# Weight differences of the seven-pass down product made in other passes, with stores and closing loads moved between queues

## The reference, cut to what matters

```python
def conv_ffn(h, w_up, conv_w, conv_b, w_down):
    u = h @ w_up
    val, gate = u[..., :FFN_HIDDEN], u[..., FFN_HIDDEN:]      # FFN_HIDDEN = 2816
    gate = depthwise_conv(gate, conv_w, conv_b)
    return (jax.nn.silu(gate) * val) @ w_down                 # [tokens, 2816] @ [2816, 1024]
```

## Time and profile before

| | |
|---|---|
| median of 3 runs | 3294.82 us (3293.86 to 3299.07) |
| the profiled execution | 3293.83 us, its span 3291.7 us |
| PE busy | 3143.3 us (95%) |
| VectorE, ScalarE, GpSimd busy | 2085.7 us (63%), 1451.2 us (44%), 666.6 us (20%) |
| mean granted clock of TensorE | 0.983 of full speed |
| DMA | 421.59 MB, mean 128 GB/s |

### The profile page before, as it was taken

The page is one execution under the profiler, slowest core; times in us unless marked ns, Lnnn a source line. Parts: engine busy times, 40 slices in busy tenths (PEclk is TensorE's granted clock), DMA queues, the critical chain, the costliest instruction groups (busy, mean ns, idle before and its releaser), DMA issues. The chain is left out here.

```text
span 3291.7 us, 48901 instructions
## 1 busy us (share of the span) xinstructions
PE 3143.3 (95%) x19182; PEld 2707.4 (82%) x19182; DVE 2085.7 (63%) x2504; ACT 1451.2 (44%) x2491; POOL 666.6 (20%) x770
## 2 busy tenths in 40 slices
PE   7999898899999999999898999999999999999897
PEld 5888777788999999777787778888887788888786
DVE  4999767556755655588544335555554676776687
ACT  5121456465332333344565325555554433333444
POOL 0001000121222222133222101111111222332233
PEclk8999999899999999999999999999999999999999
DMA  6224686533122122666633743422212232222765
GB/s 216 71 88 151 198 267 224 175 102 86 55 77 78 57 76 74 205 212 198 215 131 131 257 161 65 110 51 56 55 45 71 88 80 84 78 82 85 270 198 202
DMA packets 284052, 421.59 MB, mean 128 GB/s; under 512 B 90217, under 2 KB 188457, under 8 KB 282801
## 3 DMA queue, kind: packets, MB, share of 16 engines
q1 hardware_dynamic: 272272, 375.47, 36.8%
q0 software_dynamic: 11552, 43.01, 3.5%
HBM read 324.26 MB, written 94.13 MB: 127 GB/s over the span
## 5 line engine op out<-in xcount | busy, mean ns | idle before, releaser
L2137 DVE TENSOR_TENSOR ring_lo<-raw_rows,ring_hi 128x512 fp32r<-128x512 f32 x200 | 182.7, 914 | 203.4 <-ACT ring_hi L1995 203.1
L1281 PE MATMUL banks<-y_hi,ring_hi 128*128 128x384 f32 (+2 forms) x688 | 221.9, 323 | 4.8 <-DVEq L2125 4.0
L1283 PE MATMUL banks<-y_hi,ring_lo 128*128 128x384 f32 (+2 forms) x688 | 221.8, 322 | 0.0
L1282 PE MATMUL banks<-y_lo,ring_hi 128*128 128x384 f32 (+2 forms) x688 | 221.6, 322 | 0.0
L4584 DVE TENSOR_REDUCE mla_neg_max<-mla_scores 128x1 f32<-128x1280 f32 x128 | 190.1, 1485 | 45.6 <-PE mla_scores L90 45.6
L4554 ACT ACTIVATE mla_e<-mla_scores,mla_neg_max 128x1280 f32<-128x1280 f32 x128 | 169.9, 1327 | 110.4 <-DVE mla_neg_max L4584 110.4
L4496 PE MATMUL mla_turned<-ident,mla_e 128*128 128x128 f32 x1280 | 206.2, 275 | 1.9 <-ACT mla_pt L4562 1.3
L4496 PEld LDWEIGHTS mla_turned<-ident,mla_e 128*128 128x128 f32 x1280 | 156.1, 140 | 48.1 <-issue 11.8
L1281 PE MATMUL banks<-differences,ring_hi 128*128 128x512 f32 (+2 forms) x560 | 192.0, 343 | 3.4 <-ACT sums L2005 2.6
L1283 PE MATMUL banks<-differences,ring_lo 128*128 128x512 f32 (+2 forms) x560 | 191.8, 342 | 0.0
L1282 PE MATMUL banks<-differences,ring_hi 128*128 128x512 f32 (+2 forms) x560 | 191.8, 342 | 0.0
(11 more groups left out here) (537 smaller groups left out, 9093.1 us busy)
## 6 DMA issues: line engine op xcount, KB each, us to landing
raw_rows<-in_ffn_w_up SPq DMA_DIRECT2D x88, 512.0 KB, 3.6
da_ada_w<-in_ada_w SPq DMA_DIRECT2D x10, 4096.0 KB, 14.4
raw_rows<-in_ffn_w_down SPq DMA_DIRECT2D x66, 512.0 KB, 3.7
raw_rows<-in_ffn_w_down SPq DMA_DIRECT2D x88, 256.0 KB, 3.2
out_raw<-scratch_act SPq DMA_DIRECT2D x66, 256.0 KB, 3.7
home_hi<-scratch_act SPq DMA_DIRECT2D x55, 256.0 KB, 3.5
scratch_act<-conv_lines SPq DMA_DIRECT2D x22, 512.0 KB, 4.1
scratch_act<-out_raw SPq DMA_DIRECT2D x22, 512.0 KB, 4.5
```

What stands on the lines that cost most here:

```text
L1281: pe.matmul(out, w_hi[:, w], b_hi[:, a:a + n], start=start and k == 0, stop=False, skip_group_check=True)
L1282: pe.matmul(out, w_hi[:, w], b_lo[:, a:a + n], start=False, stop=False, skip_group_check=True)
L1283: mm = pe.matmul(out, w_lo[:, w], b_hi[:, a:a + n], start=False, stop=k == KD // 2 - 1, skip_group_check=True)
L2137: dve.tensor_tensor(blocks(begun.lo(r)), source(r), blocks(begun.hi(r)).bitcast(F32), ALU.subtract)\
```

## The change

- The difference W12 - W11 is made in P1 and not in P5: P1 loads whole rows (512 KB), P5 loads no weights. W21 minus P6's difference is made in P4 itself, in place in the loaded buffer: P3 loads 256 KB of W22, P4 loads 256 KB of W21. Weight loads of a layer's passes go from eight to seven blocks a pair. A buffer loaded in P1 is free again when GpSimd has made its difference.
- The two last activation stores are issued by GpSimd, before its differences of steps 2 and 3, with a signal of their own (`last_stored`).
- First layer: gain, gate and x loads at j = 40 and 42, one column load in each of steps 44 to 48, the column and gate products on GpSimd at j = 54 and not 33. The next weights are loaded by GpSimd: two blocks when it comes to j = 60, then one behind each of its splits, which come every fourth step from j = 72 on and not every second from 80 on.
- Second layer: the row loads at j = 45, their product at 50, one x load in each of steps 56 to 58; the first two statistics on GpSimd at j = 71 and 72.
- ScalarE's waits in the rest count half steps (`rest_done`); the copies of the c21 block to SBUF come every fourth step of the rest; homes and activation buffers lie elsewhere.

```diff
-    def load(self, sp, s, raw, first, last):
+    def load(self, eng, s, raw, first, last):
         for k in range(first, last):
             if k >= self.RING:
-                sp.wait_ge(s.next_ready, k - self.RING + 1)
-            sp.dma_start(self.place(raw, k), self.w[k * P:(k + 1) * P, :])\
+                eng.wait_ge(s.next_ready, k - self.RING + 1)
+            eng.dma_start(self.place(raw, k), self.w[k * P:(k + 1) * P, :])\
               .then_inc((s.next0_in, s.next1_in)[k % self.RING], 16)
...
+    def load_gain(self, sp):
+        sp.dma_start(self.gates[:, :], row(self.post_gain)).then_inc(self.signals.gain_in.sem, 16)
+
+    def load_column(self, sp, n):
+
+        if n < 4:
+            to, of = self.cols[:, n // 2, n % 2, :], (self.scale_rows, self.shift_rows)[n % 2][n // 2]
+        else:
+            to, of = self.gain_col[:, :], self.pre_gain
+        sp.dma_start(to, column(of), allow_slow_non_contiguous=True).then_inc(self.signals.cols_in.sem, 16)
...
-    SUMS = (P5, P6, P7, P3)
+    ACT_SUMS = (P5, P6, P7, P3)
+    WEIGHT_SUMS = (P1, P6, P7, P4)
...
+    def act_sums_upto(self, j):
+
+        return sum(self.part(i) in self.ACT_SUMS for i in range(j + 1))
+
+    def weight_sums_upto(self, j):
+
+        return sum(self.part(i) in self.WEIGHT_SUMS for i in range(j + 1))
...
-        if self.part(j) == self.P4:
+        part = self.part(j)
+        if part == self.P5:
             return None
-        return j if j < self.steps else j - self.pairs
+        return j if part == self.P1 else j - self.pairs
 
     def step_of_load(self, n):
-        return n if n < self.P4 * self.pairs else n + self.pairs
+        return n if n < self.pairs else n + self.pairs
...
-        row = 2 * q + (part in (self.P6, self.P2, self.P3))
-        if part in (self.P5, self.P3):
-            return row, 0, 2 * BANK
-        return row, BANK if part == self.P6 else 0, BANK
+        if part == self.P1:
+            return 2 * q, 0, 2 * BANK
+        return 2 * q + (part != self.P7), BANK if part in (self.P6, self.P3) else 0, BANK
...
-        if j == 14:
+        if j == 45:
             tail.load_rows(sp)
-        if j == 24:
+        if j == 55:
             tail.rows_used(sp)
-            for t in range(3):
-                tail.load_x(sp, t, self.x_old(t))
+        if 56 <= j < 59:
+            tail.load_x(sp, j - 56, self.x_old(j - 56))
...
-        if j == 18:
+        if j == 50:
             self.tail.prepare_rows(dve)
...
     def gpsimd(self, pool, s, j):
-        pass
+        for t in range(2):
+            if j == self.begins + 5 + t:
+                self.tail.post_gpsimd(pool, t)
 
     def gpsimd_end(self, pool, s):
-        for t in range(self.tiles):
+        for t in range(2, self.tiles):
...
-    EVERY = 2
-
...
-        self.first = down.steps
-        self.tile0 = 6 * down.pairs + 5
+        self.homes_free, self.stores = homes_free, stores
+        self.begins = 6 * down.pairs
+        self.splits = self.begins + 3
+        self.tile0 = self.begins + 4
...
-        if j == 3:
-            latents.load_columns(sp)
-        if j == 14:
+        if j == 40:
+            latents.load_gain(sp)
             latents.load_gate(sp, self.lines[0][:, 0:D])
+        if j == 42:
             latents.load_x(sp, self.lines[1][:, 0:D])
-        k, left = divmod(j - self.first, self.EVERY)
-        if left == 0 and 0 <= k < KD:
-            self.following.load(sp, s, self.raw, k, k + 1)
+        if 44 <= j < 49:
+            latents.load_column(sp, j - 44)
...
-        k, left = divmod(j - self.first - 2, self.EVERY)
+        k, left = divmod(j - self.splits, self.EVERY)
         if left == 0 and 0 <= k < KD:
-            if k == 0:
-                act.wait_ge(s.step_done, self.first)
             self.following.split_scalar(act, s, self.raw, k)
...
-        if j == 33:
+        if j == 54:
             latents.prepare_columns(pool)
             latents.prepare_gate(pool, self.lines[0][:, 0:D])
+        if j == 60:
+            for stored in (s.stored0, s.stored1):
+                pool.wait_ge(stored, self.stores)
+            pool.wait_ge(s.last_stored, 16 * 2 * 2)
+            self.following.load(pool, s, self.raw, 0, self.following.RING)
...
-        k, left = divmod(j - self.first - 3, self.EVERY)
+        k, left = divmod(j - self.splits - 3, self.EVERY)
         if left == 0 and 0 <= k < KD:
-            if k == 0:
-                pool.wait_ge(s.step_done, self.first)
-            self.following.split_gpsimd(pool, s, self.raw, k)
+            self.split_next(pool, s, k)
+
+    def split_next(self, pool, s, k):
+        pool.wait_ge(s.w_sum, self.homes_free(k))
+        self.following.split_gpsimd(pool, s, self.raw, k)
+        if k + self.following.RING < KD:
+            self.following.load(pool, s, self.raw, k + self.following.RING, k + self.following.RING + 1)
 
     def gpsimd_end(self, pool, s):
-        pass
+        self.split_next(pool, s, KD - 1)
...
-            if part in (down.P5, down.P6, down.P4):
-                return t_home(q)
-            return down_raw(j)[:, BANK:2 * BANK] if part == down.P3 else down_raw(j)[:, 0:BANK]
+            return t_home(q) if part in (down.P5, down.P6) else down_raw(j)[:, 0:BANK]
...
+        def store_act(eng, f, done):
+            if f // 2 < PV:
+                eng.wait_ge(s.plain_act, max(gates_done(i) for i, (f_, _) in enumerate(order) if f_ == f % 2))
+            else:
+                eng.wait_ge(s.act_done, 4 * (f // 2 - PV) + (2 if f % 2 else 4))
+            for a, n in segments:
+                eng.dma_start(act_rows[f * P:(f + 1) * P, a:a + n], conv[f % 2][:, padded(a):padded(a) + n])\
+                   .then_inc(done, 16)
...
-                    if down.part(before) == down.P3:
-                        sp.wait_ge(s.w_sum, down.sums_upto(before))
+                    if down.part(before) == down.P1:
+                        sp.wait_ge(s.w_sum, down.weight_sums_upto(before))
...
-                if j < PAIRS:
+                if j < PAIRS - 1:
                     sp.wait_ge(stored[0], 16 * len(segments) * (j + 1))
+                elif j == PAIRS - 1:
+                    sp.wait_ge(s.last_stored, 16 * 2 * len(segments))
                 elif j == PAIRS:
                     sp.wait_ge(s.step_done, 2)
-                    sp.wait_ge(stored[1], 16 * len(segments) * PAIRS)
+                    sp.wait_ge(stored[1], 16 * len(segments) * (PAIRS - 1))
...
-                if j == 3:
-                    store_act(FT - 1)
-                    store_act(FT - 2)
                 closing.sync(sp, s, j)
...
-                if part == down.P5:
-                    pool.wait_ge(s.step_done, 2)
+                if part == down.P1:
+                    pool.wait_ge(s.step_done, 1 if q < 4 else 2)
                     op = pool.tensor_tensor(home, upper, lower, ALU.subtract)
                 elif part == down.P6:
...
                 else:
-                    pool.wait_ge(s.w_sum, down.sums_upto(down.step(down.P7, q)))
-                    pool.wait_ge(s.down_lo, down.units_before(down.step(down.P6, q) + 1))
-                    op = pool.tensor_tensor(home, lower, home, ALU.subtract)
+                    pool.wait_ge(s.w_sum, down.weight_sums_upto(down.step(down.P6, q)))
+                    op = pool.tensor_tensor(lower, lower, home, ALU.subtract)
                 op.then_inc(s.w_sum, 1)
...
-                if down.summed(j):
+                if j == 2:
+                    store_act(pool, FT - 1, s.last_stored)
+                if j == 3:
+                    store_act(pool, FT - 2, s.last_stored)
+                if down.part(j) in down.WEIGHT_SUMS:
                     weight_sum(j)
                 closing.gpsimd(pool, s, j)
...
-                r = ring_at(j, i)
-                if j >= down.steps:
+                r, part = ring_at(j, i), down.part(j)
+                if part == down.P5:
+                    act.wait_ge(s.w_sum, down.weight_sums_upto(down.step(down.P1, down.at(j)[1])))
+                elif part in (down.P6, down.P7, down.P4):
+                    act.wait_ge(s.w_sum, down.weight_sums_upto(j))
+                else:
                     down_loaded(act, j)
-                    act.wait_ge(s.step_done, j - 1 if j > down.steps else j - 2)
-                elif down.part(j) in (down.P1, down.P2, down.P3):
-                    down_loaded(act, j)
+                before = down.units_before(j) + i - 4
+                if before < 0:
+                    act.wait_ge(s.step, r - 3 if r - 4 != LAST else r - 4)
+                elif before < down.steps:
+                    act.wait_ge(s.step_done, before + 1)
                 else:
-                    act.wait_ge(s.w_sum, down.sums_upto(j))
-                if j < 4:
-                    act.wait_ge(s.step, r - 3 if r - 4 != LAST else r - 4)
-                elif j < down.steps:
-                    act.wait_ge(s.step_done, j - 3)
```

(31 more changed lines are left out.)

50 lines of the change are left out of this document (15 added, 35 removed).

## The result

The changed kernel takes 3272.07 us (median of 4 runs, 3269.43 to 3274.43) against 3295.14 (3293.86 to 3299.07) beside it: ratio 0.9928, 95% interval 0.9911 to 0.9945. A second comparison, on another occasion, gave 3275.47 (6 runs) and 0.9935 (0.9922 to 0.9948). It is faster, as forecast, but by 23 us where 41 were forecast, and 1 us outside the range. The profiled execution took 3270.93, its span is 3269.1.

A forecast was written before the change was run, and what follows sets the result against it. Bound: TensorE's waits beyond 2.72 us a step, 52.5 us in all, and the lower clock behind them. Terms: 52.43 gone, 12.1 left, net 40.3; 3293.8 - 40.3 = 3253.5, median 1.0 above: 3254 us, range 3243 to 3271.

The forecast's parts named there:

- P1: Down product's first pass: "Cost 0", loses 0 (0 to 3) us instead of 9.54; step 4's weights ready at about 1352.
- P5, P6: Passes after P1, both layers: P5 loses 0.5 us instead of 14.09, P6 1.0 instead of 7.74.
- P3 with P7: Passes receiving the moved closing work, both layers: 6.0 us (0 to 14) lost, where P3 lost 7.63.
- P4: Pass given a load and a difference per step: loses 1.2 us for both layers (0 to 6).
- rest: The 22 steps ending the first layer's down product: loses 3.4 us (1.4 to 10) instead of 13.43.
- What GpSimd pays for is hidden: In the rest: GpSimd's added work costs nothing, as it is idle in most of it (19.73 busy of 73.27 us).
- The rival on collisions: Rest: transfers of next weights still collide with the step's own, keeping 10 of 13.43 us; 3261 us, chance 0.14.
- The term of the last wait: Before the rest's last steps: one split on ScalarE, one on VectorE plus hand-over, about 1.4 us for 2.64.
- VectorE has no activation sum in P4: P4: given, with P7's lossless nearest row and GpSimd catching up, for the small loss of 1.2 us.
- Slower, by the chain through GpSimd: P1 and P4: landings twice their median (7.4 us) lose 0.95 a step, 42 us; 3313 at landings of 8.6; chance 0.05.
- Nothing is won: Whole kernel: waits only pass on to the next late transfer and show again steps later; 3295 us, chance 0.03.
- P7 and P3 kept 5.3 and not 14: Rival: P7 and P3 can't hold the work moved there, 14 us left instead of 6.0; 3262 us, chance 0.16.

The follow-up runs named there:

- closing_back: Changed kernel with closing loads and row product back in their old places: first layer's P1 lost 9.8 us; second layer's P5 0.4, P6 2.3; no whole time given.
- early_diff: Changed kernel with GpSimd's differences of steps 0 to 3 no longer waiting for step 0's end: P1 lost 2.5 us for 6.0; no whole time given.
- all_fixes: Changed kernel with earlier differences, split pieces, SyncE issuing next weights, stores before reloads, later tile sums, closing work in P2: 3255.96 us, 0.9880 of the kernel before.
- all_rows: all_fixes with own places for the second layer's x rows of tiles 3 to 7, loaded in P5, no reload at the end: 3251.49 us, 0.9866 of the kernel before.
- low_pieces: Changed kernel with GpSimd's low part of the next weights cut into four pieces: rest 62.84 us, losing 3.0 for 9.4; no whole time given.
- small_next: Changed kernel with six of eight loads of next weights cut from 1056 columns to 16: rest lost 6.3 us for 9.4; no whole time given.
- post_later: Changed kernel with VectorE's sums of tiles 0 and 1 moved behind step 76 of the second layer: P4's start to the end 59.1 us for 54.1.
- all_fixes_late: all_fixes with the splits of the next weights from step 76, one in three steps: 3256.55 us, 0.9878 of the kernel before.

## Why the prediction was right in sign and off in size

Three terms were too small: P1, P4 and the rest. In the rest and P4, and in part in P1, the step that failed is the same: the sum counted a GpSimd instruction in GpSimd's time alone. By its own terms (left after the change, forecast and measured):

| term | forecast | measured | miss |
|---|---|---|---|
| P1 | 0 | 6.0 | +6.0 |
| P5, P6 | 1.5 | 0.0 | -1.5 |
| P3 with P7 | 6.0 | 5.3 | -0.7 |
| P4 | 1.2 | 6.3 | +5.1 |
| rest | 3.4 | 9.4 | +6.0 |
| end behind the last matmul | no change | 19.5 for 16.9 | +2.6 |

Together +17.5, and 40.3 - 17.5 = 22.8 is the gain of the profiled executions, 3293.83 - 3270.93 = 22.9 (the down product's later start, 1.1, about cancels against the few tenths left out of the terms).

**P5 and P6** were right for the stated reason: no load and no difference in P5. closing_back bears it out.

**P1, "Cost 0".** The step that failed is the load of step 4. The prediction had the weights of step 4 as the first to wait for a difference; those of step 3 wait too, for the difference of step 0. They left at 1346.83, and landing took 6.5 at the median, not 3.7, since weights and stores now ran together behind one late start. The weights of step 4, forecast to leave at 1346.1 and be ready at about 1352, left at 1348.53, behind two differences that took 3.53 and not 2.6, and step 4 began at 1357.71. early_diff shows the cause in the first layer, where 3.5 is left for a bound of 3. For P1 of the second layer the sum has no term at all: it went from 0.1 to 2.5, and early_diff explains the lesser part of that, 0.7.

**P7 and P3** came out near the forecast, but the reason is not shown. closing_back brings the two passes to 0.2 and all_fixes to 0.0, but all_rows, which has no closing load there either, loses 3.3, and without any edit of them they lose from 1.4 to 6.4. What sets this stays open, so that 5.3 came near 6.0 is partly luck.

**The rest, 3.4.** The step that failed is "What GpSimd pays for is hidden". The sign stood in the earlier trace rows already: a longest VectorE split of 2608 ns beside a median of 682, and the earlier trace rows have a GpSimd split of 2.46. That GpSimd is idle most of the time says nothing of what its instruction does to VectorE. low_pieces takes 6.4 of the 9.4 away without a byte less. The rival on collisions forecast a loss near this size for another reason, and it has a share: the middle waits, 4.6, go as well with fewer bytes or with later loads. The term of the last wait (1.4 for 2.64) was wrong too, by the same step: 3.30 before the row of 1625.60. The edits put the last of GpSimd's splits beside the last group's, where the kernel before has none. From ScalarE's row at 1622.40 to VectorE's at 1624.67 go 2.27 us, where ScalarE's 0.63 would do, so without that split the wait would be 3.30 - 1.64 = 1.7, an estimate from these rows and near the 1.4 (not tried; the pieces still leave 2.7). And a long wait isn't always followed by the lower clock, as the prediction took it from the stretches before: behind 3.3 us the last 24 matmuls ran at 1.00 in the changed kernel and at 0.76 in small_next.

**P4, 1.2.** "VectorE has no activation sum in P4" is true, but GpSimd's differences take VectorE's time as well: it is busy 32.98 of 34.65 us there. A split of the second layer's P4, in the changed kernel and in the one before:

```profile
3221.48 1.77 DVE L2300 TENSOR_TENSOR ring_lo<-raw_rows,ring_hi 128x512 fp32r<-128x512 f32 x1
```

```profile
3250.84 0.69 DVE L2280 TENSOR_TENSOR ring_lo<-home_hi,ring_hi 128x512 fp32r<-128x512 f32 x1 [0.83 <-ACT ring_hi L2075]
```

That alone costs little: with VectorE held in most steps (1.18 to 1.78), but the sums of tiles 0 and 1 out of the way, post_later's P4 loses 0.4. The sums alone cost little too: the kernel before has them at the same steps and loses 0.4. Together they make the 4.7. In the first layer P4 loses 0.0 in all_fixes_late, where GpSimd has one split in it and not three, and 1.8 in all_fixes. Besides, in the second layer the sum counted the wrong thing. TensorE's loss in P4 was not on the path that sets the end. On it were VectorE's first sums and SyncE's loads of step 76 ahead of the first store; the ring of rows then sets the pace. 47.2 us became 54.1: 6.9, which is the 4.3 by which P4 loses more, and the 2.6 at the end; by the path, the first store leaves 4.9 later, and the rest of the way takes 2.0 more.

**The rivals.** Slower, by the chain through GpSimd, didn't come: the weights' median landings, 5.6 and 5.3 in the two P1 and 3.4 and 2.6 in the two P4, stayed below the 7.4 at which it decides. "Nothing is won" didn't either, and P7 and P3 kept 5.3 and not 14.

## What to carry to other kernels

Price a GpSimd instruction with two SBUF inputs at its whole length on VectorE as well, wherever VectorE is busy (here 2.6 us for 0.68), and look for VectorE instructions of the same form with a maximum far above the median. When two runs of a stage differ, compare TensorE's waits and its granted clock before the length. For each buffer that gets another reader ask of every load behind it, the first included, what it now waits for. When the matmuls in front of an end get shorter, work out what else ends there: a store, a reload and the next store in one queue can be the path, and a wait of TensorE then costs nothing.

## What the runs showed of the hardware that was not expected

Four GpSimd pieces back to back let VectorE in between (0.84 to 1.25 each, 3.98 for the four), but three whole differences back to back did not: VectorE's split took 4.71 beside 3.77, though its row begins 0.39 us ahead of theirs. The row comes again in all_fixes and all_rows. Which of the two is the rule, and what parts them, was not tried. Nor is it known why the clock falls behind the same wait in one run and not in another.
